# Decoder trunk step: sample states in whole 8 KB runs, a quarter of a head per partition

## The reference

```
dt  = softplus(dtr + dt_bias);  a = -exp(a_log)
S'[b,h,p,n] = S[b,h,p,n] * exp(dt[b,h]*a[h]) + (x[b,h,p]*dt[b,h]) * B[b,g,n]      # g = h // 8
y[b,h,p]    = sum_n S'[b,h,p,n] * C[b,g,n] + d_skip[h] * x[b,h,p]
y = y * silu(z);  y = y * rsqrt(mean over group of y*y + eps) * g_ssm
m = sigmoid(gA) * (o_att @ w_pa) + sigmoid(gB) * (y @ w_pb);  x += gate1 * (m @ w_o)
```

## Time and profile before

| | |
|---|---|
| median of 3 runs | 876.09 us |
| the profiled execution | 877.11 us, its span 875.5 us |
| busy, share of the span | PE 91%, PE weight load 63%, DVE 43%, ACT 35%, POOL 14% |
| DMA | 219.4 MB, mean 251 GB/s |
| mean granted PE clock | 0.955 of full |

### The profile page before, as it was taken

One profiled execution on the slowest core, in us unless ns is written; L12 is line 12 of the kernel. 1 busy time (PEld: TensorE's weight loads), 2 busy tenths in 40 slices (PEclk: granted clock), 3 DMA queues, 4 the chain that ended last, 5 costly groups with the idle time before them and its releaser, 6 DMA issues. The chain is left out here.

```text
span 875.5 us, 12751 instructions
## 1 busy us (share of the span) xinstructions
PE 793.7 (91%) x4637; PEld 551.7 (63%) x4637; DVE 372.5 (43%) x936; ACT 304.8 (35%) x733; POOL 120.2 (14%) x148
## 2 busy tenths in 40 slices
PE   3889989999997899998999629999959999999996
PEld 3466778777785576888888428888633443444433
DVE  2364627565564056574994670111311221212212
ACT  1232147555564146654945400101311221212213
POOL 4320000000000110521545530000000000000000
PEclk9999989999999999999999868999959999999999
DMA  9794433837566413228889799446549999999992
GB/s 296 251 351 154 143 115 131 310 121 265 158 231 214 147 48 108 68 91 282 270 274 280 233 328 394 140 144 241 199 164 421 423 424 422 425 422 424 423 418 69
DMA packets 107407, 219.42 MB, mean 251 GB/s; under 512 B 9288, under 2 KB 81472, under 8 KB 95028
## 3 DMA queue, kind: packets, MB, share of 16 engines
...
## 5 line engine op out<-in xcount | busy, mean ns | idle before, releaser
L1587 PE MATMUL bank<-h_normed,weight_ring 128*128 128x264 f32 x1024 | 241.5, 393 | 2.3 <-ACT arena L867 2.3
L1587 PEld LDWEIGHTS bank<-h_normed,weight_ring 128*128 128x128 f32 x1024 | 194.4, 193 | 39.5 <-issue 4.2
L1898 PE MATMUL bank<-arena,h_normed 128*64 128x512 f32 x176 | 79.8, 608 | 0.0
L1820 PE MATMUL bank<-y_T,weight_ring 128*128 128x264 f32 x256 | 60.3, 400 | 3.9 <-DVE y_T L1366 3.9
L1820 PEld LDWEIGHTS bank<-y_T,weight_ring 128*128 128x128 f32 x256 | 50.5, 198 | 13.2 <-issue 4.0
L1898 PE MATMUL bank<-weight_ring,h_normed 128*64 128x512 f32 x192 | 56.3, 594 | 0.6 <-ACT h_normed L997 0.6
L1446 DVE TENSOR_TENSOR arena<-arena,bank 128x512 f32<-128x512 f32 x8 | 8.7, 1091 | 105.2 <-PE bank L1898 105.2
L1453 DVE SCALAR_TENSOR_TENSOR x_residual<-bank,modulation,x_residual 128x256 f32<-128x256 f32 x64 | 28.8, 484 | 56.7 <-PE bank L1939 56.7
L1520 PE MATMUL bank<-identity,arena 128*128 128x128 f32 (+5 forms) x236 | 32.8, 280 | 18.9 <-ACT arena L804 9.3
L946 ACT ACTIVATE arena<-arena,expanded 128x128 f32<-128x128 f32 x128 | 38.3, 387 | 33.1 <-DMA arena<-bc_scratch 23.6
L1334 DVE SCALAR_TENSOR_TENSOR arena<-arena,expanded 128x128 f32<-128x128 f32 x128 | 37.9, 373 | 21.5 <-DMA arena<-in_state_ssm 21.3
...
...
## 6 DMA issues: line engine op xcount, KB each, us to landing
...
arena<-in_w_down SPq DMA_DIRECT2D x11, 1024.0 KB, 26.8
...
```

The source lines that it names most:

```text
L1587: ins = mm(ps[:, 0:T], w, hT[:, c, :], start=c == 0, stop=c == KD - 1)
L1820: ins = mm(ps[:, 0:T], w, yT[:, c, :], start=c == 0, stop=c == NXB - 1)
L1898: ins = mm(banks[i][BLK * e:BLK * e + BLK, :], xg[:, 4 * h + c, BLK * e:BLK * e + BLK], ws[e][:, c, :], start=h == 0 and c == 0, stop=h == ...
```

## The change

A state is laid out with (head, quarter of its rows) on the partition: partition 4h+f holds rows 16f to 16f+15 of head h, 2048 numbers that are one run of 8 KB in DRAM. All of a partition belongs to one head, so the decay is one number per partition for the whole state and B/C are the same for its 16 rows. Hence: one B/C tile for all samples (`bc`, 32 partitions per group, 4 DMAs), x and the decays come through DRAM scratches into this layout (`x2`, `dq`), the update is two operations of 1024 columns, there are three state buffers, POOL's queue stores the states, and y goes back to the channel layout through a scratch (new job `ys`). `ssm(b)` stands ahead of every second job of the merged list, and `yn` ahead of `sw`. The list is now

```diff
-        s_odd, bc_odd, prod = part(NXB * NST), part(2 * SG * NST), part(NXB * NST)
-        s_even, bc_even, bx = part(NXB * NST), part(2 * SG * NST), part(NXB * NST)
+        st1, st2 = part(NXB * NST), part(NXB * NST)
+        prod_lo = part(NXB * NST // 2)
+        st0 = part(NXB * NST)
+        prod_hi, bx = part(NXB * NST // 2), part(NXB * NST)
+        y2 = part(NXB * NS).rearrange("p (l b) -> p l b", b=NS)
+        sst, prod = (st0, st1, st2), (prod_lo, prod_hi)
...
-            if i % 3 == 2 and i // 3 < NS:
-                jobs += [("ssm", i // 3)]
+            if i % 2 == 0 and i // 2 < NS:
+                jobs += [("ssm", i // 2)]
             jobs += [j]
-        jobs += [("sw",), ("yn",)]
+        jobs += [("ys",), ("yn",), ("sw",)]
...
-        st_d = t["state_ssm"].rearrange("o b (c h) p n -> (o b) (h p) c n", h=2)
+        st_d = t["state_ssm"].rearrange("o b h (f p) n -> (o b) (h f) (p n)", f=4)
...
                 if s == ("pb", 0, 0):
-                    store_states(NS - 2)
-
-                    for i in range(2):
-                        sp.wait_ge(st_full[i], 16 * (NS // 2))
+                    for i in range(3):
+                        sp.wait_ge(st_full[i], 16 * len(range(i, NS, 3)))
                 if before[s]:
-                    done_jobs = jobs[:jobs.index(last_user[before[s]])]
-                    store_states(sum(j[0] == "ssm" for j in done_jobs))
...
+            pool.wait_ge(bs_out, 64)
+            pool.dma_start(x2, sx_d.rearrange("(q l) b -> q l b", l=NXB)).then_inc(x2_in, 16)
+            for f in range(4):
+                pool.dma_start(dq[f:128:4, :], se_d).then_inc(x2_in, 16)
...
             def load_state(b):
-                if b >= 2:
-                    pool.wait_ge(st_prod, b - 1)
-                pool.dma_start(bc[b % 2], bc_d[b:b + 1, :].to_broadcast([128, 2 * SG * NST]))\
-                    .then_inc(bc_full[b % 2], 16)
-                if b >= 2:
-                    pool.wait_ge(st_out[b % 2], 16 * (b // 2))
-                pool.dma_start(sst[b % 2].rearrange("p (c n) -> p c n", c=NXB), st_d[b]).then_inc(st_full[b % 2], 16)
+                if b >= 3:
+                    pool.wait_ge(st_out[b % 3], 16 * (b // 3))
+                pool.dma_start(sst[b % 3], st_d[b]).then_inc(st_full[b % 3], 16)
...
             for b in range(NS):
                 pool.wait_ge(st_new, 2 * b + 2)
+                pool.dma_start(so_d[b], sst[b % 3]).then_inc(st_out[b % 3], 16)
                 if b:
                     pool.wait_ge(st_red, b)
...
+                    if b + 2 < NS and b + 2 > 2:
+                        load_state(b + 2)
+                for q in range(4):
+                    ins = g.tensor_tensor(prod[q // 2][:, 512 * (q % 2):512 * (q % 2) + 512].rearrange("p (l n) -> p l n", l=4),
+                                          sst[b % 3][:, 512 * q:512 * q + 512].rearrange("p (l n) -> p l n", l=4),
+                                          bc[:, b, 1:2, :].to_broadcast([128, 4, NST]), ALU.mult)
                 ins.then_inc(st_prod, 1)
...
+            pool.wait_ge(y2_ready, 1)
+            pool.dma_start(sy_d.rearrange("(q l) b -> q l b", l=NXB), y2).then_inc(y2_out, 16)
+            pool.wait_ge(y2_out, 16)
+            pool.dma_start(yT[:, :, NP:T], sy_d.rearrange("(c p) b -> p c b", p=128)).then_inc(y2_in, 16)
...
-                        act.dma_start(bc_d, wdf[0:NS, 0:2 * SG * NST]).then_inc(bs_out, 16)
+                        rows = wdf[0:NS, 0:2 * SG * NST].rearrange("b (k g n) -> b k g n", k=2, g=SG)
+                        for q in range(2):
+                            act.dma_start(bc_d.rearrange("g (b k n) -> b k g n", b=NS, k=2)[:, q], rows[:, q]).then_inc(bs_out, 16)
+                        act.wait_ge(u_ready, NCB)
+                        act.dma_start(sx_d.rearrange("(c p) b -> p c b", p=128), u[:, 0:NXB, NP:T]).then_inc(bs_out, 16)
+                        act.wait_ge(fd_sp, 1)
+                        act.dma_start(se_d, ex[:]).then_inc(bs_out, 16)
...
                 elif k == "cb":
                     ps = filled(dve, j)
+                    if j[1]:
+                        dve.wait_ge(x2_in, 16 * 5)
+                        link(v.tensor_tensor(xdt, x2, dq[:, 0:NS].unsqueeze(1).to_broadcast([128, NXB, NS]), ALU.mult), xds_ready)
...
                     if a == 0 and b == 0:
-                        dve.wait_ge(bs_out, 16)
+                        dve.wait_ge(bs_out, 64)
...
-                    for c in range(NXB):
-                        if c % 8 == 0:
-                            dve.wait_ge(bx_ready, 2 * b + 1 + c // 8)
-                        x = sst[b % 2][:, NST * c:NST * c + NST]
-                        ins = v.scalar_tensor_tensor(x, x, exo[:, c, NS + b:NS + b + 1], bx[:, NST * c:NST * c + NST],
-                                                     ALU.mult, ALU.add)
-                        if c % 8 == 7:
-                            ins.then_inc(st_new, 1)
+                    for h in range(2):
+                        dve.wait_ge(bx_ready, 2 * b + 1 + h)
+                        x = sst[b % 3][:, 1024 * h:1024 * h + 1024]
+                        v.scalar_tensor_tensor(x, x, dq[:, NS + b:NS + b + 1], bx[:, 1024 * h:1024 * h + 1024],
+                                               ALU.mult, ALU.add).then_inc(st_new, 1)
...
                 for e in range(2):
...
-                    pe.wait_ge(moe_full[s], (r * moe_uses(s) + use) * 16)
+                    if e == 0:
+                        pe.wait_ge(moe_full[s // 2], (r * moe_uses(s) + use) * 32)
```

109 lines of the change are left out of this document (56 added, 53 removed).

## The result

| us | before | after |
|---|---|---|
| median of 16 runs | 872.87 (869.04 to 878.14) | 878.25 (870.91 to 881.09) |
| ratio of the two, 95% interval | | 1.0044 (1.0024 to 1.0064) |
| profiled execution, its span | 877.11, 875.5 | 875.1, 873.7 |
| `g0` starts | 406.37 | 413.55 |
| first C product (POOL) starts | 420.71 | 425.37 |

The change is slower by 0.44%, 3.8 us with an interval of 2.1 to 5.6 (the two medians are 5.4 apart); 859 us were predicted. That forecast was a gain of 17.1 us from the median of three runs, 876.09; from 872.87 it would be 855.8. The two profiled executions lie near opposite ends of their kernels' spread, so their spans alone would mislead. I compare intervals from `g0`, the first gate job: in profiles of code that is the same up to there, `g0` started anywhere between 401.9 and 406.8 us.

What follows compares the result with a forecast made beforehand. Bound: PE up to the experts, kept waiting by the chain of eight states, then expert-weight transfer. `pb` from 524.9 to 509.6 gains 15.3, plus 3.1 of clock: 877.1 − 18.4 = 858.7, so 859 us; range 849 to 872.

Steps and rivals of the forecast that it cites:

- Step 5: DVE's wait for x and decays at `cb(1)`: 9.6 us late there, +3.5 us for everything behind, bounds 1.5 and 9.6.
- Step 4: Start of state 0, now ahead of `g0` and `yp0`: first update done about 7 us after `g0` starts, before 14.3.
- Step 7: Cycle from state to state: 9.4 us, 11 where a `yp` stands between, three of six; y complete at 498.3.
- Step 8: y's way through the scratch: 7.1 us added, bounds 5 and 13; PE's `pa` ends at 506, `pb` starts at 509.6.
- 3.1 us of clock behind `pb`: First 128 `pb` products: PE barely idles ahead of them, so the lower clock's 3.1 us come back.
- step 1: State and B/C transfers: 8 KB runs save some 25 us of DMA time before 500; no landing waits with three buffers.
- step 2: SP's queue no longer holds gate and `pa` weights behind a state; weights are in time in both kernels: nothing.
- step 3: State update on DVE: two operations of 1024 columns, 2.6 against 4.29 us; the sum in two halves 2.35.
- A: Rival, more gain: shared port and `yp` cost nothing, cycle 8.4 us in all six, PE's work bounds; 851 us, chance 0.12.
- B: Rival: DVE's update blocks POOL in full, 2.6 instead of 1.0 us per cycle, 1.7 per `yp`; 867 us, chance 0.14.
- C: Rival, not faster: DMA still sets the state's pace, 12 us per state at 293 GB/s; 877 to 880 us, chance 0.08.
- D: Rival, slower: a late-landing store holds the load ahead of a product in POOL's queue, cycle 14 us; 885 us, chance 0.06.

Runs made afterwards that it cites:

- e1: Changed kernel with a state again behind every third gate or `pa` job instead of ahead of every second; 878.57 us, ratio 1.0044 to the kernel before.
- a2: Second profile of the changed kernel, no edit; the profiled execution took 874.41 us.
- e3: Changed kernel with x and decays loaded early and a state behind every third job; 871.26 us, ratio 0.9963 to the kernel before.
- e5: e2 with the states ahead of jobs 0, 3, 6 and so on; 867.84 us, ratio 0.9952 to the kernel before.
- e8: e3 with ACT's fourth prompt-state store issued behind the first 16 x·dt·B products; 871.08 us, ratio 0.9982 to the kernel before.
- e9: e2 with ACT's late store, `sw` ahead, states ahead of eight listed jobs, `yp` jobs between the `fs` jobs; 863.29 us, ratio 0.9889 to the kernel before.
- e12: e5 with `sw` ahead of `ys` and `yn`; 866.34 us, ratio 0.9903 to the kernel before.
- e2: Changed kernel with the five loads of x and decays behind POOL's first big product instead of its third; 870.23 us, ratio 0.9956 to the kernel before.

## Why the prediction was wrong

In us; "after" are the two profiles, "before" the means of the three.

| | before | predicted | after |
|---|---|---|---|
| `g0` later by | | 3.5 | 7.8 (mean 412.6 of after, e1, a2; 404.8 of five with the old head) |
| `g0` to first product | 14.3 | 7.1 | 11.8, 10.6 |
| first to eighth product | 89.8 | 73.3 | 75.9, 75.7 |
| `g0` to y complete | 112.1 | 88.4 | 95.5, 94.1 |
| y complete to y landed | | 7.1 | 6.8, 7.5 (9.1 to 9.7 in e1, e3, e5, e8, e9, e12) |
| `g0` to the end of the last `pa` | 99.5 | 96.1 | 106.8, 106.3 |
| y complete to `pb` | 5.7 | 11.3 | 16.5, 17.4 |

The ledger by measured numbers: the chain of states is 17.3 us shorter, 11.3 go for what now stands between y and `pb`, 7.8 for the head, so `pb` is 1.8 later. That answers why the 18 us of gain are missing. It does not account for the 3.8 us of loss: from `pb` to the first expert product the changed kernel took 122.2 and 122.7 us, the one before 123.9, 124.6 and 125.7, and from there to the end 226.0 against 226.3 to 226.7. Its profiles are not slower than those of the kernel before, its timed runs are, and which stretch holds the 3.8 us is not shown.

- **Step 5, the wait at cb(1), failed in size.** The wait itself was predicted at 9.6 and DVE is late by that much (351.45 to 361.28). That the engines behind it would catch up, all but 3.5 us of it, was wrong: I looked at DVE's and ACT's idle third, but PE was full from 350 to 375 (25.00 of 25 us in e2 and the kernel before), and in the changed kernel it lost 3.5 us of it and more behind. A full engine has nothing to catch up with. The true price, 7.8 us, lay near the upper bound of 9.6; taking the wait away in e2 gave 7.7 us of time back.
- **Step 4, the first state, failed by 3.5 to 4.7 us.** The sum had no term for ACT's issue of the fourth store, 0.39 us in the kernel before. It took 3.92 and 2.65 us, one to one ahead of the first product: 7.9 us plus the issue in each of six profiles, where 7.1 were predicted in all. What keeps the issue that long is not settled (last section).
- **Step 7, the cycle, was right where no `yp` stands** (9.5 of 9.4) **and up to 1 us short where one does** (12.06, 12.03 and 11.26 of 11). The mechanism was put on the wrong engine: I let DVE stretch POOL's product, while POOL's product holds DVE's `yp` operations to its own end, so DVE's own sum became the cycle. The earlier trace rows already had it: DVE's four operations end at 439.59 and POOL's product at 438.91. Over seven intervals that is 2.5 us.
- **Step 8 failed in PE's term, and held in the trip's.** "The banks hold PE back some 4 us" was 17.7: PE's jobs took 106.8 us from `g0` instead of the 89.1 of e1, since ACT reads a bank only behind its part of the next state. (The recorded end of `pa` at 506 allows 7 us and not 4; it makes no difference.) That is 5 to 6 us more between y and `pb` than forecast. The trip took 6.8 and 7.5 us of 7.1, and y had to wait for PE. Where PE does not stall the trip grows to 9.1 to 9.7, its store landing beside `pb` weights, and would have put `pb` at nearly the same place (e1).
- **The 3.1 us of clock behind `pb` came back in part:** the first 128 products took 29.91 and 30.13 us, against 31.62, not 28.5. The other two profiles of before have 30.63 and 31.38, e2 has 31.38, so only about 1 us of it stands out from the scatter.
- **Right:** step 1, no landing wait left, and 309 GB/s over 425 to 475; step 2; step 3, the update, 2.48 against 2.6 predicted; step 6; and that a gain or loss ahead of `pb` reaches the end one to one (e2: 7.7 of 7.0 to 8.3).
- **The rivals.** A fell. B's condition, POOL held for the updates' whole length of 2.6 us in each cycle, occurred in part (6.24 and 7.01 for 4.95, in three of eight products); its mirror image cost more. C fell: the pace was not set by DMA, 268 GB/s at 77% busy from 475 to 500 is no limit. D fell: no wait for a store stood in POOL's queue. POOL's issues of the stores took 0.54 to 0.58 us, so no run here shows the shortage of descriptors of which the Trainium skill warns ("SBUF — State Buffer", Who interferes with whom). What happened, four undersized terms along one chain (4.3 us for `g0`, 3.5 to 4.7 for the first state, 2.5 for the cycles, 5 to 6 for PE's banks), was in no rival. The range's upper end, 872, missed the median by 6.
